# Attention loops of a hybrid encoder trunk: scores two pairs ahead, exponentials between the copies, normalisation with spread sums, and moved low-half splits

## What is computed

```python
def _dsa_mixer(...):                    # layers 0 and 3
    q, k, v, qi, ki, wi = jnp.split(h @ w_in, ...)
    q, k, qi, ki = _rope(...)           # rotary on each
    dots = relu(einsum('bthd,bsd->bths', qi, ki_all))         # 8 indexer heads
    score = einsum('bth,bths->bts', wi, dots) * iscale        # summed over the heads
    sel = lax.top_k(score, top)                               # the best keys per row
    logits = einsum('btkgd,btskd->btkgs', qg, kg) * scale     # 16 heads
    prob = softmax(logits)
    o = einsum('btkgs,btskd->btkgd', prob, vg)
    return o @ w_out
def _mla_mixer(...):                    # layer 2: 16 heads of 64 + 32 rotary
    prob = softmax((qn . k_nope + qp . kpe) * scale);  o = prob . v;  return o @ w_out
def _rwkv7_mixer(...):                  # layer 1
    k = k * (1 + (a - 1) * k_a); ...
    bonus = jnp.sum(hs(r) * hs(k) * r_k, axis=-1, keepdims=True) * hs(v)
```

## Time and profile before

| | |
|---|---|
| median of 3 runs | 1799.29 us (1799.11 to 1801.41) |
| profiled execution, its own time | 1800.91 us |
| its span in the profile | 1799.1 us |
| mean granted TensorE clock | 0.966 of 2.4 GHz |
| PE busy | 1678.7 us (93%) |
| DVE busy | 1173.9 us (65%) |
| ACT busy | 855.7 us (48%) |
| POOL busy | 717.5 us (40%) |

### The profile page before, as it was taken

The page is one execution under the profiler, slowest core; times in us unless marked ns, Lnnn a source line. Parts: engine busy times, 40 slices in busy tenths (PEclk is TensorE's granted clock), DMA queues, the critical chain, the costliest instruction groups (busy, mean ns, idle before and its releaser), DMA issues.

```text
span 1799.1 us, 37483 instructions
## 1 busy us (share of the span) xinstructions
PE 1678.7 (93%) x14117; PEld 1592.1 (88%) x14117; DVE 1173.9 (65%) x2069; ACT 855.7 (48%) x1600; POOL 717.5 (40%) x801
## 2 busy tenths in 40 slices
PE   7978999996988997999999988999999997999997
PEld 6857999994778997999999877999999885999997
DVE  4775777737477455577755647577764586677743
ACT  3444566433653433465633444465643445556532
POOL 5641566400035110366611354266621760466600
PEclk9998999998999998999999998899999998999999
DMA  7313555454231002455555211355546511555453
GB/s 199 105 34 95 140 153 150 125 150 126 78 110 30 5 9 79 139 142 150 138 145 172 86 50 48 107 151 147 149 129 160 157 49 48 141 140 156 125 146 95
DMA packets 344896, 205.09 MB, mean 114 GB/s; under 512 B 22456, under 2 KB 342184, under 8 KB 344656
## 3 DMA queue, kind: packets, MB, share of 16 engines
q1 hardware_dynamic: 342640, 199.76, 38.8%
q0 software_dynamic: 2144, 3.77, 0.8%
HBM read 200.02 MB, written 3.39 MB: 113 GB/s over the span
## 4 chain that ended last, share of the span: by engine, by line
PE 80%; DVE 11%; ACT 5%; issue 3%; POOL 1%; DMA 0%; SPq 0%; DVEq 0%; ACTq 0%; POOLq 0%
PE bank L877 23%; PE bank L878 23%; PE bank L879 23%; PE bank L1205 4%; DVE lo L1984 2%; PE bank L888 1%; ACT hi L1495 1%; ACT LS L1528 1%; DVE LS L2036 1%; DVE LS L2027 1%; DVE SC L2160 1%; PE bank L938 1%; PE bank L1229 1%; PE bank L1144 1%; POOL lo L666 1%
## 5 line engine op out<-in xcount | busy, mean ns | idle before, releaser
L877 PE MATMUL bank<-XH,hi 128*128 128x320 f32 (+1 forms) x1992 | 630.3, 316 | 15.8 <-DVE lo L1984 7.7
L1984 DVE TENSOR_TENSOR lo<-raw,hi 128x2048 fp32r<-128x2048 f32 (+3 forms) x201 | 428.7, 2133 | 309.5 <-ACT hi L1495 309.5
L878 PE MATMUL bank<-XL,hi 128*128 128x320 f32 (+1 forms) x1992 | 621.4, 312 | 0.0
L879 PE MATMUL bank<-XH,lo 128*128 128x320 f32 (+1 forms) x1992 | 621.4, 312 | 0.0
L877 PEld LDWEIGHTS bank<-XH,hi 128*128 128x128 f32 (+1 forms) x1992 | 377.4, 189 | 30.2 <-DVE lo L1984 10.4
L1495 ACT ACTIVATE hi<-raw 128x2048 fp32r<-128x2048 f32 (+4 forms) x205 | 359.8, 1755 | 74.6 <-PE bank L879 65.1
L878 PEld LDWEIGHTS bank<-XL,hi 128*128 128x128 f32 (+1 forms) x1992 | 377.9, 190 | 1.3 <-issue 0.2
L879 PEld LDWEIGHTS bank<-XH,lo 128*128 128x128 f32 (+1 forms) x1992 | 377.4, 189 | 0.0
L702 POOL TENSOR_TENSOR upad<-upad,rstd 128x128 f32<-128x128 f32 (+1 forms) x176 | 167.7, 973 | 199.8 <-ACT upad L1574 199.8
L877 PE MATMUL bank<-GH,hi 128*128 128x322 f32 x704 | 219.8, 312 | 3.6 <-DVE lo L1984 3.6
L878 PE MATMUL bank<-GL,hi 128*128 128x322 f32 x704 | 218.7, 311 | 0.0
(11 more groups left out here) (379 smaller groups left out, 2436.0 us busy)
## 6 DMA issues: line engine op xcount, KB each, us to landing
raw<-in_f_w_up SPq DMA_DIRECT2D x176, 512.0 KB, 5.0
raw<-in_f_w_down SPq DMA_DIRECT2D x64, 704.0 KB, 4.7
raw<-in_a_w_in SPq DMA_DIRECT2D x12, 1024.0 KB, 5.3
raw<-in_b_w_rkv SPq DMA_DIRECT2D x12, 1024.0 KB, 5.1
raw<-in_a_w_out SPq DMA_DIRECT2D x8, 1024.0 KB, 5.2
raw<-in_b_w_out SPq DMA_DIRECT2D x4, 1024.0 KB, 5.3
raw<-in_c_w_out SPq DMA_DIRECT2D x4, 1024.0 KB, 5.1
raw<-in_a_w_in SPq DMA_DIRECT2D x12, 256.0 KB, 4.8
```

The source lines that it names most:

```text
L877: pe.matmul(out, a, xh(k), start=(start and k == 0), stop=False)
L878: pe.matmul(out, a, xl(k), start=False, stop=False)
L879: last = pe.matmul(out, b, xh(k), start=False, stop=(stop and k == kt - 1))
L1984: dve.tensor_tensor(lo[n % 2][:, 0:w_], raw[n % 2][:, 0:w_], hi[n % 2][:, 0:w_].bitcast(F32), ALU.subtract).then_inc(w_lo, 1)
```

## The change

In the attention loops of DSA and MLA the order of a pass changes on three engines. PE does `pair_qk(p+2)` first, then `turn_probs(p)` and `values(p)`. DVE does `maxima(p+2)` first, then `pt_copy(p)`, `probs(p+1)`, `out_lo(p)` (with the swaps of MLA's heads between `pt_copy` and `probs`). ACT does `exps(p+2)` between `pt_copy(p)` and `out_hi(p)`. In DSA `project(15)` and `project(16)` now stand between the scores of pairs 0 and 1 and behind them, ACT's `evac(15)` and `evac(16)` follow `exps(0)` and `exps(1)`, and DVE does `probs(0)` ahead of `maxima(1)`.

`probs` multiplies with three TENSOR_TENSOR operations, whose second input is the reciprocals spread by a stride of zero, in place of five TENSOR_SCALAR. The first head's three products into `SC` and the 128 x 384 mask become SCALAR_TENSOR_TENSOR with a constant column spread the same way (for the mask the value OFF, a new column of the constants).

Slab 5's low half in DSA moves from DVE to POOL, ahead of POOL's eight query ropes. POOL's DMA of the mask moves ahead of all four pieces of slab 7's low half. In RWKV the low halves of slabs 10 and 11 move to earlier places on DVE, and the bonus sums of block 3 move from tile 20 to tile 21.

```diff
@@ -45,7 +45,7 @@
-CONSTS = [("ident", 128), ("ones", 128), ("eps", 3), ("headsum", 128), ("pairsum", 32), ("pairfan", 128), ("place", 96),
+CONSTS = [("ident", 128), ("ones", 128), ("eps", 4), ("headsum", 128), ("pairsum", 32), ("pairfan", 128), ("place", 96),
           ("place_rot", 96), ("cos_a", T), ("sin_a", T), ("cos_c", T), ("sin_c", T), ("valid0", 128),
@@ -54,7 +54,7 @@
 NCONST = _n
-FIRST_CONSTS = 259
+FIRST_CONSTS = 260
@@ -130,7 +130,7 @@
     put("scan_keep", keep)
-    put("eps", np.broadcast_to(np.array([EPS, 64e-5, 0.0], np.float32), (128, 3)))
+    put("eps", np.broadcast_to(np.array([EPS, 64e-5, 0.0, OFF], np.float32), (128, 4)))
     return c
@@ -829,15 +829,15 @@
                         store(dst[2], KIo[0:n_, z, :])
+                    split_lo(first_slab[layer, "mix"] + 5, 0, 4)
                     for p in range(PAIRS):
                         rope(R0[layer] + 7 + p, E0[layer] + 9 + p + 1, cosr[:, :], sinr[:, :], QD[:, p, :])
                         if p == 0:
                             split_lo(first_slab[layer, "mix"] + 6, 0, 4)
                         if p == 1:
-                            split_lo(first_slab[layer, "mix"] + 7, 0, 2)
                             pool.wait_ge(mask_done, 2 * inst + 1)
                             pool.dma_start(MK[64:128, 384:576], MK[0:64, 384:576]).then_inc(mask_copied, 16)
-                            split_lo(first_slab[layer, "mix"] + 7, 2, 4)
+                            split_lo(first_slab[layer, "mix"] + 7, 0, 4)
                     squares(norm_of[layer, "ffn"])
@@ -1106,16 +1106,15 @@
                 pair_qk(0)
+                project(15)
                 pair_qk(1)
-                project(15)
+                project(16)
                 for p in range(PAIRS):
-                    turn_probs(Q + p)
                     if p + 2 < PAIRS:
                         pair_qk(p + 2)
+                    turn_probs(Q + p)
                     g = slice(64 * (p // 4), 64 * (p // 4) + 64)
                     values(Q + p, lambda e: (Vc[:, g], Vt[0:64, 0, g], Vt[:, 1, g], Vt[:, 2, g]))
-                    if p == 0:
-                        project(16)
                 mixer_out(layer, lambda k: OH[:, k, :], lambda k: OL[:, k, :], lambda: pe.wait_ge(ol_done, Q + PAIRS))
@@ -1166,7 +1165,7 @@
                 fans_at = {12: (0, 1), 13: (2, 3, 4), 14: (5, 6, 7)}
-                bonus_at = {18: (0,), 19: (1,), 20: (2, 3), 21: (4,), 22: (5, 6), 23: (7,)}
+                bonus_at = {18: (0,), 19: (1,), 20: (2,), 21: (3, 4), 22: (5, 6), 23: (7,)}
                 for i in range(24):
@@ -1697,15 +1696,14 @@
                 exps(Q)
+                evac(15)
                 exps(Q + 1)
-                evac(15)
+                evac(16)
                 for p in range(PAIRS):
                     pt_copy(Q + p)
-                    out_hi(Q + p, p)
                     if p + 2 < PAIRS:
                         exps(Q + p + 2)
-                    if p == 0:
-                        evac(16)
+                    out_hi(Q + p, p)
                     if p == 4:
@@ -2032,9 +2030,12 @@
                 chain(dve.reciprocal(rsum[:, slot(q), 0:5], sums[:, slot(q), 0:5]))
-                for u, (a, b) in enumerate(UNITS):
-                    ins = dve.tensor_scalar(LS(q)[:, a:b], LS(q)[:, a:b], rsum[:, slot(q), u:u + 1], None, ALU.mult)
-                ins.then_inc(prob_done, 1)
+                heads = LS(q)[:, 0:768].rearrange("p (e n) -> p e n", e=2)
+                for first, a, b in ((0, 0, 128), (1, 128, 384)):
+                    r_ = rsum[:, slot(q), first:first + 3:2].rearrange("p (e o) -> p e o", o=1).to_broadcast([128, 2, b - a])
+                    dve.tensor_tensor(heads[:, :, a:b], heads[:, :, a:b], r_, ALU.mult)
+                dve.tensor_tensor(LS(q)[:, 768:960], LS(q)[:, 768:960], rsum[:, slot(q), 4:5].to_broadcast([128, 192]), ALU.mult
+                                  ).then_inc(prob_done, 1)
@@ -2144,7 +2145,6 @@
                 dve.tensor_copy(KIT[:, 0:PAST], psum[3][:, 256:384]).then_inc(turned_in, 1)
-                split_lo(s0 + 5)
@@ -2155,7 +2155,8 @@
                         if h == 0:
-                            ins = dve.tensor_scalar(SC[0:n_, a:b], relu[0:n_, 0, a:b], w_, None, ALU.mult)
+                            ins = dve.scalar_tensor_tensor(out=SC[0:n_, a:b], in0=relu[0:n_, 0, a:b], scalar=w_,
+                                                           in1=C("eps", n_)[:, 2:3].to_broadcast([n_, b - a]), op0=ALU.mult, op1=ALU.add)
                         else:
@@ -2178,21 +2179,22 @@
                         dve.tensor_scalar(MK[0:64, 384:576], SW[0:64, 384:576], -3.0e38, OFF, ALU.is_gt, ALU.mult).then_inc(mask_done, 1)
-                dve.tensor_scalar(MK[:, 0:384], SW[:, 0:384], -3.0e38, OFF, ALU.is_gt, ALU.mult).then_inc(mask_done, 1)
+                dve.scalar_tensor_tensor(out=MK[:, 0:384], in0=SW[:, 0:384], scalar=-3.0e38, in1=C("eps")[:, 3:4].to_broadcast([128, 384]),
+                                         op0=ALU.is_gt, op1=ALU.mult).then_inc(mask_done, 1)
                 dve.wait_ge(mask_done, 2 * inst + 2)
                 dve.wait_ge(mask_copied, 16 * (inst + 1))
                 masks = [MK[:, 0:128], MK[:, 128:384], MK[:, 0:128], MK[:, 128:384], MK[:, 384:576]]
                 maxima(Q, masks, A_SCALE)
                 swap(Rb + 11, E + 14, SWAP_A)
+                probs(Q)
                 maxima(Q + 1, masks, A_SCALE)
                 swap(Rb + 12, E + 15, SWAP_A)
-                probs(Q)
                 for p in range(PAIRS):
+                    if p + 2 < PAIRS:
+                        maxima(Q + p + 2, masks, A_SCALE)
                     pt_copy(Q + p)
                     if p + 1 < PAIRS:
                         probs(Q + p + 1)
-                    if p + 2 < PAIRS:
-                        maxima(Q + p + 2, masks, A_SCALE)
                     if p < 2:
@@ -2318,14 +2320,13 @@
                 keys_and_rows(1)
+                split_lo(s0 + 10)
                 bonus(0)
                 keys_and_rows(2)
-                split_lo(s0 + 10)
                 bonus(1)
+                split_lo(s0 + 11)
                 keys_and_rows(3)
                 for m in range(2, KD):
-                    if m == 3:
-                        split_lo(s0 + 11)
                     bonus(m)
@@ -2500,16 +2501,16 @@
                 for p in range(PAIRS):
+                    if p == 0:
+                        dve.wait_ge(stored, 16 * STORES_AT["latent"])
+                    if p + 2 < PAIRS:
+                        maxima(Q + p + 2, masks, C_SCALE)
                     pt_copy(Q + p)
                     if 2 * p + 7 < 16:
                         head(2 * p + 6)
                         head(2 * p + 7)
                     if p + 1 < PAIRS:
                         probs(Q + p + 1)
-                    if p == 0:
-                        dve.wait_ge(stored, 16 * STORES_AT["latent"])
-                    if p + 2 < PAIRS:
-                        maxima(Q + p + 2, masks, C_SCALE)
                     out_lo(Q + p, p)
```

## The result

The changed kernel takes 1813.25 us (median of 4 runs, 1808.67 to 1813.86) against 1799.54 for the kernel before in the same comparison: ratio 1.0065, 95% interval 1.0048 to 1.0082. It is slower by 0.65%, some 12 us, which is clear of the noise though small. The forecast was 1800.5 and no change; the range ended at 1807.

A forecast was written before the change was run, and what follows sets the result against it. PE held 80% of the chain, its idle time in the attention stretches being about all the loops could gain. 2 x 0.3 (DSA) + 2.7 (MLA) - 2.3 (RWKV) = +1.0 on 1800.91; median forecast 1800.5 us, range 1788 to 1807.

The forecast's parts named there:

- The new order closes a ring over POOL: MLA loop: copy, ropes, scores, maxima, next copy make passes of 10.15 us against 9.44, +2.8 for four.
- The term MLA: Whole MLA loop, passes, tail and entry together: +2.7 us, bounds -2.5 and +7.
- The tail has no ropes and gains 0.6: End of MLA's loop: without ropes there, it gets 0.6 us shorter.
- the seven passes' -3.4: DSA loop: steady passes of 4.75 us against 5.22, -0.48 each, -3.4 over seven.
- each piece lets one score operation by: DSA, slab 5 on POOL: four score sums take 5.0 us, not 1.5; net +3.3, bounds -0.6 and +3.5.
- the slower rival: POOL keeps the port over several boundaries in DSA, ropes are held in MLA: 1808; whole or part, chance 0.31.
- the whole would be wrong if the clock left 0.84 to 0.86 by 0.05 or more: PE's granted clock in the attention stretches: such a shift would move its 147 us of busy time by some 7.
- what can be won is what DVE's waits hold: RWKV, bound by DVE: at most 4.7 us, from waits of 2.4 us for each of the first two bonuses.
- Of this I take half: RWKV: half the possible gain is counted, -2.3 us, bounds 0 and -4.7.
- the new forms gain only by being three and not five: DVE's spread multiplications: they contend with POOL too, so only their smaller number gains.
- the first rival: Spread forms don't wait for POOL: -10.9 us, 1788.4; with its weaker forms and the third rival, chance 0.36.
- the rule: Port shared by DVE and POOL: two-SBUF-input DVE instructions contend with POOL's SBUF reads; two-port ones lock out for a whole instruction.

The follow-up runs named there:

- E2: Changed kernel with DVE's two swaps of the later pair ahead of the maxima in the MLA loop: 1790.54 us, ratio 0.9945 to the kernel before.
- E11: Changed kernel with only DVE and ACT back in the old order in MLA's loop, PE keeping the new one: 1806.11 us, ratio 1.0011 to the kernel before.
- E5: Changed kernel with DVE's low halves of slabs 8 and 9 in MLA's loop waiting for the pass's last rope: 1805.21 us, ratio 1.001 to the kernel before.
- E1: Changed kernel with MLA's loop in its old order on PE, DVE and ACT: 1800.18 us, ratio 1.0004 to the kernel before.
- E4: Changed kernel with five TENSOR_SCALAR per pair again, new order kept: 1800.66 us, ratio 1.0003 to the kernel before.
- E6: Changed kernel with a semaphore wait of POOL on itself between the pieces of its low halves: 1815.48 us, ratio 1.0063 to the kernel before.
- E3: Changed kernel with slab 5's low half back on DVE, ahead of the score sums: 1808.89 us, ratio 1.0031 to the kernel before.
- E7: Kernel before with only the RWKV part of the change: 1799.71 us, ratio 0.9981 to the kernel before.
- E8: Changed kernel with slab 5 on DVE, mask copy between slab 7's pieces and MLA's swaps first: 1784.5 us, ratio 0.9891 to the kernel before.
- E12: E8 with the mask's copy ahead of all four pieces of slab 7: 1787.74 us, ratio 0.9915 to the kernel before.

## Why the prediction was wrong

**The sum failed at MLA, and the sign with it.** The step "The new order closes a ring over POOL" was right: passes without a low half take 9.8 us (forecast 10.15), PE waits for QT ahead of L908, and E2 and E11 confirm the ring. (The terms given for it, 5.8 + 1.8 + 1.5 + 0.8, add up to 9.9, not 10.15.) The term MLA was +2.7 and measured +8.6: +0.8 up to the first copy (forecast +0.5), +6.0 in the four passes (+2.8), +1.8 behind them (-0.6). What was mis-sized:

- *The low halves in the ring.* The forecast took one mean of 9.44 us per pass and never asked what stands in the second and fourth. That mean is of passes of 7.4 and of 11.3 to 11.7. The ring of 9.8 makes the short ones 2.4 us longer each; the long ones have room for it (10.0 and 10.5 in E5, where the split waits for the rope). But in the changed kernel DVE's split meets there a rope on which the scores wait, and they take 12.4 and 11.7. Of the 2.6 us by which the second exceeds a pass without a low half, the rope's last operation has 1.4; behind it the granted clock was 0.72 (1084 to 1090 us). With the split held back (E5) the four passes cost 2.4 us, near the +2.8 of the forecast; the meeting costs the other 3.6. It needs both parts of the change (E1, E4), which no price of single edits would have given.
- *The tail.* The step "The tail has no ropes and gains 0.6" failed: it does have them, since the last scores wait for the last ropes, 4.2 us, one pass later than I had counted. From the fifth copy to the output projection it is 1136.49 - 1110.73 = 25.8 us where it was 23.3: +2.5.
- *The clock.* The forecast let the clock be as before. In the tail it was at 0.50 from 1117 us to the output projection, and E5, which got the higher level back, is 3.9 us shorter there. This is the price against E5, whose tail of 21.9 us, with a wait as long, is also 1.4 shorter than the 23.3 of the kernel before. The kernel before ran much of its own tail at the lower level (0.60 from 1120 to 1137 us), so the clock's share of the +2.5 is not shown; it is no further term beside the +2.5.

**DSA came nearly as worked out, in layer 0.** Passes of 4.81 us (4.75), the loop -6.5 (-5.6; of it the seven passes' -3.4 is -3.3 by its own numbers), first exponentials at 106.72 (105.5), first copy at 115.75 (114.1), layer 0 at +0.7 (+0.3). Where it missed, the step was "each piece lets one score operation by": one waited for three of them (4.46 us). In E6, with gaps between the pieces, it is as the step has it. The selection began 4.45 us late, beyond the bound of +3.5. In E3, with slab 5 back on DVE, that wait is gone. This is what the slower rival had named, that the port stays with POOL over several boundaries, for the mask operation's 3.27 us of the earlier trace rows; I had it in the rivals and not in the sum. Layer 3 is at +2.9: there the first copy comes 9.3 us later against the layer's start (forecast 5.9), the loop being 6.3 shorter; why it is 1.5 us more than in layer 0 no run shows. The forecast had also said that the whole would be wrong if the clock left 0.84 to 0.86 by 0.05 or more. In both DSA stretches it did, to 0.91 and 0.90. The higher clock can only have helped, and how much of the loops' gain is its doing no run separates.

**RWKV.** "what can be won is what DVE's waits hold" and "Of this I take half": -1.8 in the changed kernel's trace, but -0.4 in E7 and -0.2 to -1.4 in most others. So the near hit of -1.8 for -2.3 is partly luck. PE's wait moved to the next key block (3.9 us in both kernels), and the clock was lower from 560 to 570 us, 0.83 in the changed kernel and 0.66 in E7 for 0.98.

**The form.** "the new forms gain only by being three and not five": wrong in MLA, where being done sooner put the split ahead of the rope. The spread ones wait too: two of them take 2.07 us beside the ropes of MLA (from 1078.40) and 1.03 in layer 0's loop, so the first rival (no contention) is excluded. One reading behind the rule was too broad: L2002 took 0.83 us or more in four cases of 56, where POOL was at its squares or began them at once, and its usual 0.55 in the rest, nearly all of which began 0.1 us before an operation of POOL; and the multiplications of the earlier trace rows took three times their 1.24 us, not twice. Of the slower rival, 1808 where 1813 came out, the mechanism in DSA was right (the port stays with POOL over several pieces). In MLA it was right in sign and size but not in mechanism: it held the ropes up at each of the multiplications, and what held them was the split. So it came near partly by luck.

**The end, +2.3,** is in no step. It is there in most kernels (E8 to E12 too) and absent in E1, E4 and E6. It goes with the clock: the last 27 us have 0.88 in the kernels at 0.0, 0.84 or 0.85 in E2 and E7 (+1.5), and 0.77 or 0.78 in those at +2.3 to +2.6. E7 has the old code there, so no edit is needed for it. What sets the clock there stays open.

## What to carry to other kernels

When an order is changed so that a loop runs further ahead, write down the ring of waits that the new order closes, with every engine in it, and put into it whatever else stands in those passes on those engines, pass by pass and not as a mean. A cheap producer that feeds the next scores (here two swaps of 0.5 us) belongs ahead of the long wait, not behind it: moving them gained 20 us in MLA where the change had lost 9. Price edits in pairs where they share an engine: here each of two was harmless alone. And take a mean only of passes that are alike.

## What the runs showed of the hardware

- A DVE operation with two SBUF inputs, beside GpSimd operations that follow each other at once, waited for several of them: 4.46 us through three pieces, 5.14 us through the rest of the pieces and two operations of a rope. With a semaphore wait between the pieces it took at most 1.55 and 1.20 us. The Trainium skill, page "SBUF — State Buffer", section "Who interferes with whom", says that the pair is held for the whole instruction; by that rule the wait would end with the piece. Here the mask operation ended in both layers only behind GpSimd's next gap (0.08 us, between two operations of a rope), and the score operation of 4.46 us between the third and the fourth piece, where the profile shows no gap. So the wait lasted longer than by the rule, and the measurement decides.
- The other way round, GpSimd's operations of 0.86 us took 2.25 to 2.78 us beside a DVE split of 2.0 to 2.6 us.
- PE's granted clock in the last passes of MLA was 0.50 behind a wait of 4.2 us and 1.00 in E2, where no wait there exceeded 1.6 us. In E5 it was 0.53 from 1108 to 1117 us around a wait of 4.1 us and 1.00 from 1120 to 1128: a wait of this length went with the lower level, but not with how long it stayed.
